# Gate and up products with the tokens as loaded operand and 512 weight columns moving, in a float32 transformer and expert kernel on one core

## The reference

```python
def swiglu(h, w_gate, w_up, w_down):
    return (jax.nn.silu(h @ w_gate) * (h @ w_up)) @ w_down

h = rms_norm(x, norm_g[l, 0])
x = x + 0.5 * swiglu(h, ffn_w_gate[l, 0], ffn_w_up[l, 0], ffn_w_down[l, 0])
```

## Time and profile before

| | us |
|---|---|
| median of 3 runs | 2014.35 |
| lowest, highest run | 2012.62, 2015.29 |
| span of the profiled execution | 2012.0 |
| PE busy, share | 1960.5, 97% |
| DVE busy, share | 1176.1, 58% |
| ACT busy, share | 702.8, 35% |

### The profile page before, as it was taken

How to read it: one execution, slowest core, us unless ns; L and a number is a source line. 1 busy time by engine, 2 the same in 40 slices (tenths; PEclk the granted TensorE clock), 3 DMA queues, 4 the chain that set the end, 5 groups by cost and what they waited for, 6 DMA issues and landing times.

```text
span 2012.0 us, 34328 instructions
## 1 busy us (share of the span) xinstructions
PE 1960.5 (97%) x14457; PEld 1630.7 (81%) x14457; DVE 1176.1 (58%) x2009; ACT 702.8 (35%) x1052; POOL 0.2 (0%) x4
## 2 busy tenths in 40 slices
PE   9999999999999999999999999999899999989997
PEld 9999998889999999999888999999675544444443
DVE  6666659876655765575987757657755422222212
ACT  5433536535333533343653534343322000000001
POOL 0000000000000000000000000000000000000000
PEclk9999999999999999999999999999999999999999
DMA  7799563376776677656325676644318999999995
GB/s 242 243 355 254 173 185 106 118 213 195 219 220 198 208 216 222 193 175 192 116 95 176 207 224 195 206 110 126 126 34 344 401 420 421 421 421 421 421 421 234
DMA packets 274100, 476.17 MB, mean 237 GB/s; under 512 B 28198, under 2 KB 234080, under 8 KB 249368
## 3 DMA queue, kind: packets, MB, share of 16 engines
q1 hardware_dynamic: 273692, 473.85, 68.4%
q10 hardware_dynamic: 252, 0.08, 0.0%
HBM read 472.75 MB, written 7.95 MB: 239 GB/s over the span
## 4 chain that ended last, share of the span: by engine, by line
PE 83%; DMA 11%; DVE 4%; ACT 1%; issue 0%; DVEq 0%; ACTq 0%
PE ps L764 82%; DMA ring_zone<-in_moe_w_up_dram 7%; DMA ring_over<-in_moe_w_up_dram 3%; DMA hT<-in_moe_w_up_dram 1%; PE ps L1095 1%; PE ps L1238 0%; DVE PT L2292 0%; DVE WL L1941 0%; PE ps L1404 0%; DVE xT L2698 0%; DVE hl L1881 0%; ACT mT L1723 0%; ACT gT L1671 0%; DVE gT L2321 0%; DVE gT L2326 0%
## 5 line engine op out<-in xcount | busy, mean ns | idle before, releaser
L1870 DVE TENSOR_TENSOR WL<-W,WH 128x1024 fp32r<-128x1024 f32 x390 | 473.0, 1223 | 310.2 <-ACT WH L1488 309.5
L764 PE MATMUL ps<-hh,WH 128*128 128x256 f32 x2232 | 633.4, 284 | 1.3 <-DVE WL L1870 0.7
L764 PE MATMUL ps<-hh,WL 128*128 128x256 f32 x2232 | 622.6, 279 | 0.0
L764 PE MATMUL ps<-hl,WH 128*128 128x256 f32 x2232 | 622.5, 279 | 0.0
L1488 ACT ACTIVATE WH<-W 128x1024 fp32r<-128x1024 f32 x390 | 408.1, 1055 | 450.1 <-PE ps L764 422.6
L764 PEld LDWEIGHTS ps<-hh,WH 128*128 128x128 f32 x2232 | 418.8, 188 | 14.8 <-issue 11.6
L764 PEld LDWEIGHTS ps<-hl,WH 128*128 128x128 f32 x2232 | 418.4, 187 | 1.2 <-issue 1.0
L764 PEld LDWEIGHTS ps<-hh,WL 128*128 128x128 f32 x2232 | 419.2, 188 | 0.0
L764 PE MATMUL ps<-hid_h,WH 128*128 128x256 f32 x704 | 200.8, 285 | 0.0
L764 PE MATMUL ps<-hid_l,WH 128*128 128x256 f32 x704 | 196.5, 279 | 0.0
L764 PE MATMUL ps<-hid_h,WL 128*128 128x256 f32 x704 | 196.5, 279 | 0.0
(11 more groups left out here) (391 smaller groups left out, 2565.4 us busy)
## 6 DMA issues: line engine op xcount, KB each, us to landing
W<-in_ffn_w_gate_dram SPq DMA_DIRECT2D x88, 512.0 KB, 4.9
W<-in_ffn_w_up_dram SPq DMA_DIRECT2D x88, 512.0 KB, 4.6
W<-in_ffn_w_down_dram SPq DMA_DIRECT2D x88, 512.0 KB, 4.0
W<-in_w_in_dram SPq DMA_DIRECT2D x78, 512.0 KB, 4.6
ring_over<-in_moe_w_gate_dram SPq DMA_DIRECT2D x28, 1024.0 KB, 25.1
ring_over<-in_moe_w_up_dram SPq DMA_DIRECT2D x28, 1024.0 KB, 25.7
ring_over<-in_moe_w_down_dram SPq DMA_DIRECT2D x28, 1024.0 KB, 26.6
W<-in_w_gate_dram SPq DMA_DIRECT2D x48, 512.0 KB, 3.6
```

Of the source, the lines that this page charges most:

```text
L764: ins = nc.tensor.matmul(o, lhsT, rhs, start=start, stop=stop, skip_group_check=True, **kw)
L1870: v.tensor_tensor(low, W[:, i % RAW, :], high.bitcast(F32), ALU.subtract).then_inc(low_ready, 1)
```

## The change

In an FFN the tokens are now the loaded operand of the gate and up products (128 of them at a time, `tt`), and 256 gate columns beside 256 up columns, which lie in two neighbouring places of `WH` and `WL`, are the moving one: 512 columns, one bank for each half of the tokens. The order of pieces in a block becomes gate, up (first half of the width), gate, up (second half). SiLU with the token factor as its scale on ACT and one DVE operation for each half of the tokens make the hidden block with tokens on the partitions; four transposes on PE turn it back into the second bank, between the two halves of the down product of the block before; ACT copies the high part from there, DVE subtracts the rest. The ada products and the others stand behind the transposes. Square root and reciprocal are now of two columns. ACT and DVE split pieces up to fixed numbers (`split_to`).

```diff
+def block_at(b):
+    return 6 * b - 2 if b else 0
...
-                add("ffn_gate", key, b)
-                add("ffn_up", key, b)
+                plan.extend((kind, key, b, half) for half in range(2) for kind in ("ffn_gate", "ffn_up"))
...
+            def rows_of_strips():
+                pe.wait_ge(part_ready, due(part_ready))
+                for tt in range(TT):
+                    mm(ps[:, 1, tt:tt + 1], rs[:, tt * P:(tt + 1) * P], ones[:, 0:1], tt == 0, tt == 1,
+                       then=sum_ready if tt else None)
...
+            def gate_and_up(banks, half, h_wait, then):
+                slot = split_no[st["taken"]] % PAIRS
+                take("ffn_gate")
+                take("ffn_up")
+                for j in range(4):
+                    k = 4 * half + j
+                    if h_wait:
+                        pe.wait_ge(h_ready, due(h_ready))
+                    w = (WH[:, slot:slot + 2, j * 256:(j + 1) * 256], WL[:, slot:slot + 2, j * 256:(j + 1) * 256])
+                    for tt in range(TT):
+                        mm3(banks[tt], h_at(k, tt * P, P), w, k == 0, k == KD - 1, then=then if k == KD - 1 else None)
+                done_pair(2)
+            def turn_hidden_rows(b, bank):
+                pe.wait_ge(hid_rows, due(hid_rows))
+                for f in range(2):
+                    for tt in range(TT):
+                        ins = nc.tensor.transpose(bank[:, f * T + tt * P:f * T + (tt + 1) * P],
+                                                  hid_f[:, b % 2, tt, f * P:(f + 1) * P], ident)
+                ins.then_inc(hid_turned, 1)
...
+                for b in range(FF_BLOCKS):
+                    banks = [begin()]
+                    turns.step()
+                    banks.append(begin())
+                    split_hidden[b] = turns.step()
+                    gate_and_up(banks, 0, b == 0, None)
+                    if b == 0:
+                        squares_by_strip()
+                    if b == 1:
+                        turn_hidden_rows(0, last)
+                    gate_and_up(banks, 1, b == 0, work_ready)
+                    if b == 0:
+                        rows_of_strips()
+                    else:
+                        dve_did(split_hidden[b - 1])
+                        down(b - 1, 0)
+                        turn_hidden_rows(b, banks[1])
+                        side_products(l, i, b)
+                        down(b - 1, 1)
...
 ACT
+                for b in range(FF_BLOCKS):
+                    n = n0 + block_at(b)
+                    split_to(n + 4)
+                    if b == 0:
+                        strips_out()
+                    if b == 1:
+                        hidden_high(0)
+                    split_to(n + 6)
+                    if b == 0:
+                        row_root()
+                        act.wait_ge(row_factor, 2 * l + i + 1)
+                    for tt in range(TT):
+                        bank = look()
+                        turned_bank[b] = turns.bank()
+                        nc.scalar.activation(sg[:, b % 2, tt, :], bank[:, 0:T], ACT.Silu,
+                                             scale=rstd_of[:, tt:tt + 1]).then_inc(sg_ready, 1)
+                        turns.step()
+                    if b:
+                        split_to(n + 7)
+                        hidden_high(b)
+                        split_to(n + 8)
                     if (l, i, b) == (0, 0, LATE_BLOCK + 1):
                         set_up()
...
 DVE
+                for b in range(FF_BLOCKS):
+                    n = n0 + block_at(b)
+                    split_to(n + 4)
+                    if b == 1:
+                        hidden_low(0)
+                    split_to(n + 6)
+                    if b == 0:
+                        row_factors()
+                    for tt in range(TT):
+                        bank = take() if tt == 0 else ps[:, WORK + (turns.n) % WORK, :]
+                        turned_bank[b] = turns.bank()
+                        dve.wait_ge(sg_ready, due(sg_ready))
+                        ins = v.scalar_tensor_tensor(out=hid_f[:, b % 2, tt, :], in0=bank[:, T:2 * T],
+                                                     scalar=rstd_of[:, tt:tt + 1], in1=sg[:, b % 2, tt, :],
+                                                     op0=ALU.mult, op1=ALU.mult)
...
+                    if b:
+                        split_to(n + 7)
+                        hidden_low(b)
+                        split_to(n + 8)
```

More of the change, by code:

```diff
@@ L910, in late_vectors @@
                 turns.step()
-            def ffn(l, i):
[L914 to L949, removed]
@@ new lines, in turn_hidden_rows, with down @@
+            def turn_hidden_rows(b, bank):
[5 more added lines that the diff above has]
+                ins.then_inc(hid_turned, 1)
+            def down(c, f):
+                w = take("ffn_down")
+                hid = at((hid_h[:, c % 2, :], hid_l[:, c % 2, :]), f * T, T)
+                for n in range(KD):
+                    mm3(ps[:, n // 2, (n % 2) * T:(n % 2 + 1) * T], at(w, n * P), hid,
+                        c == 0 and f == 0 and n % 2 == 0, False)
+                done_pair()
@@ new lines, in side_products @@
+            def side_products(l, i, b):
+                if (l, i, b) == (0, 0, LATE_BLOCK):
+                    late_vectors()
+                if ada_unit(l, i, b) is not None:
+                    if ada_unit(l, i, b) == 0:
+                        pe.wait_ge(act_setup, 3)
+                    ada_rows(ada_unit(l, i, b))
+                if ada_unit(l, i, b - 1) is not None:
+                    ada_columns(ada_unit(l, i, b - 1))
+                if (l, i, b) == (1, 1, CONTEXT_AT + 1):
+                    turn_context()
+                if (l, i, b) == (1, 1, CONTEXT_AT + 2):
+                    pe.wait_ge(lrow_ready, 1)
+                    bank = begin()
+                    mm(bank[:, 0:40], ones[0:1, :], lrow[:, :], True, True, then=work_ready)
+                    turns.step()
@@ new lines, in ffn @@
+            def ffn(l, i):
+                last, split_hidden = None, {}
+                for b in range(FF_BLOCKS):
[17 more added lines that the diff above has]
+                        down(b - 1, 1)
+                    last = banks[1]
+                side_products(l, i, FF_BLOCKS)
@@ L1523, in root, with row_root @@
                     .then_inc(rms, 1)
+            def row_root():
+                act.wait_ge(sum_ready, due(sum_ready))
+                nc.scalar.activation(rstd_of[:, :], ps[:, 1, 0:TT], ACT.Sqrt, bias=eps[:, :], scale=1.0 / (32 * D))\
+                    .then_inc(rms, 1)
             def split_to(n):
@@ L1530, in split_to @@
                     high, _, before = split_place(st["split"])
-                    act.wait_ge(pair_used, before + 1)
+                    if before >= 0:
+                        act.wait_ge(pair_used, before + 1)
                     nc.scalar.activation(high, W[:, i % RAW, :], ACT.Copy).then_inc(high_ready, 1)
@@ L1590, in ffn, with hidden_high @@
             def ffn(l, i):
-                for b in range(FF_BLOCKS):
-                    used(2)
+                n0 = st["used"]
+                def hidden_high(b):
+                    act.wait_ge(hid_turned, due(hid_turned))
+                    bank = ps[:, turned_bank[b], :]
+                    nc.scalar.activation(hid_h[:, b % 2, :], bank, ACT.Copy).then_inc(hid_high, 1)
+                turned_bank = {}
+                for b in range(FF_BLOCKS):
+                    n = n0 + block_at(b)
[13 more added lines that the diff above has]
+                                             scale=rstd_of[:, tt:tt + 1]).then_inc(sg_ready, 1)
+                        turns.step()
+                    if b:
+                        split_to(n + 7)
+                        hidden_high(b)
+                        split_to(n + 8)
                     if (l, i, b) == (0, 0, LATE_BLOCK + 1):
                         set_up()
[L1595 to L1604, removed]
                     if (l, i, b) == (0, 0, LATE_BLOCK):
@@ L1614, in ffn @@
                         turns.step()
[L1615 to L1616 removed]
                 turns.step(ada_unit(l, i, FF_BLOCKS - 1) is not None)
[L1618 removed]
+                st["used"] += FFN_PIECES
+                split_to(st["used"] + 2)
             def rows(tile, at, n, src):
```

44 lines of the change are left out of this document (24 added, 20 removed).

## The result

The changed kernel takes 2038.23 us (median of 4 runs, 2036.09 to 2040.13) against 2014.54 of the kernel before in the same job: ratio 1.012, interval 1.0105 to 1.0134. It is 23.7 us slower, where 12.6 faster was forecast.

The account below looks back on a forecast made before the run. TensorE (PE), busy for 97% of the span, was taken as the bound. Terms -41.4 + 19.2 + 1.2 + 4.1 + 4.3 = -12.6 us took the span from 2012.0 to 1999.4; forecast 2001.8 us, 0.6% faster, range 1994 to 2018.

Parts of the forecast that it names:

- Term 1: FFN gate and up products: a 512-column matmul takes 0.216 us for two of 0.1178, 2112 times, -41.4 us.
- rival (a): Gate and up products: the wide matmul gains nothing, 0.236 us each, deciding from 0.222; 2043 us, slower; chance 0.12.
- Term 2: Four PE transposes per FFN block turn the gate-up product: 0.44 us a group, 44 groups, +19.2 us.
- rival (d): PE transposes take their full duration, 0.27 us each, 1.09 per group: +28.8, 2030.6 us, slower; chance 0.03.
- Term 3: Row sums: one fp32 product of 256 columns becomes two of 1 column, +0.3 us four times, +1.2 us.
- Term 4: PE waits for splits in FFN blocks: 0.6 plain, 1.2 at b=1, 1.5 behind set_up, 0.4 on two context blocks; +4.1 us.
- rival (b): Every block waits for turned copy, split and rest, ada blocks too, 0.3 us on 38 or more: 2014, no change; chance 0.13.
- Term 5: Kernel start: first matmul needs both pieces, at 17.0 instead of 13.18; 2.8 us head start lost, +4.3 us in sum.

Follow-up runs that it names:

- the run with one: The changed kernel with one PE transpose per block instead of four, three quarters of the hidden block then holding other numbers: 2024.81 us, ratio 1.0051 to before.
- the earlier start: The changed kernel with both first pieces split ahead of the rounding of x, on ACT and DVE: 2033.85 us, ratio 1.0091 to the kernel before.

## Why the prediction was wrong, point by point

**Term 1 failed**, at the sentence "So I take 0.216". The matmul of 512 columns takes 0.2333; 2112 x (0.2353 - 0.2333) = -4.3 us in place of -41.4. The missing 37.1 is as much as the whole error of 36.4 between the forecast and the measured time. Three things were wrong in it. "Two costs run side by side" left open what a narrow matmul pays beyond the larger of them and took it to vanish at 512 columns. The runs show that a change of weights adds nothing at 512 columns (0.2266, and 0.227 with one tile); and by my estimate float32r pays above its columns there too. What the columns alone take I work out from two stretches at a granted clock of 0.50: 512 columns came 0.427 apart at after's start, and 256 came 0.213 apart in before's trace from 1412.17 to 1414.94. If the distance there goes with the clock, 512 columns take 0.213 at 1.00 (0.417 ns each), my lower bound. The row I chose was of another kind, float32, whose record of 512 columns comes at twice 0.215; float32r pays 13 to 20 ns over 0.213 (0.2267 and 0.2333). And my own pointed to the right answer: the first distance of a float32r row of 128 columns, 0.058 to 0.063 in the trace and 0.06 as shown, is 0.45 to 0.49 ns a column, 0.232 or more at 512. I read it wrongly twice. I put it down to the weights being the same tile; but PE loads that tile again, and within the row the next pair on one tile is 0.11 apart, as the loads are. All 32 such short distances stand behind a 256-column matmul, so I take them for what the columns cost without the load; that is my reading of these times, no run shows it by itself. And I set the 0.06 against rival (a), though four times 0.06 is close to that rival's 0.236, and ranked the float32 row above it "in array time and in weights".

What came is rival (a), "the wide matmul gains nothing", given 0.12: 0.2333 is past its deciding point of 0.222, and its 2043 was 5 us high. The doubt it rested on, something paid per column that I couldn't name, was the better argument.

**Term 2**, +19.2: right. 0.44 a group in after's rows, and 0.10 to 0.11 per transpose by the run with one; rival (d) falls.

**Term 3**, +1.2: 0.1. The new sums lengthen PE's row by 0.45 for each FFN, from the product before them to the second behind; the old one did by 0.43.

**Term 4**, +4.1: 4.8, near by luck. 2.8 of it is 0.32 + 1.17 + 0.42 + 0.68, and 0.2 more at a wait in the context's products that the kernel before has too. Plain blocks and `set_up` came near what was worked out (0.3 and 1.5 forecast), blocks with an ada product don't wait, so rival (b) falls. But the four waits at b=1 (1.2) did not come, and the three in block 0 (2.0), which the prediction put at nothing, did: the same need for two split pieces at once that it saw at the very start holds at the second half product too.

**Term 5**, +4.3: mis-sized. No run shows the 1.5 that this sum has beside the 2.8; in its place after's start had 12 matmuls at a granted clock of 0.50, 0.427 apart instead of 0.2333, which cost 2.3. PE's first product came at 17.80, not 17.0: with the head start of 2.8 that is 5.9, and undoing it put the trace 6.3 ahead (the median 4.4).

The terms as measured give -4.3 + 19.2 + 0.1 + 4.8 + 5.9 = 25.7. The narrow matmuls that remain take back 1.8: their mean is 0.1171 for 0.1177 in the down products (1.2 us) and 0.1169 for 0.1171 in the attention products with x moving (0.6); why they shift so isn't shown. That leaves 23.9, and after's trace is 24.6 behind at the end of the last FFN, so all but 0.7 is accounted for. The span rose by only 22.8 because in before's trace the last transposes have an idle of 1.67 us among them and then run at a granted clock of 0.50 (2003.1 to 2004.9), and in after's there is neither (1.00 from 2024.9 to 2027); the change doesn't touch them. PE's timelines of before, then of after:

```profile
2003.09 1.75 PE L1461 MATMUL ps<-C,xT 128*128 128x128 f32 x7 [1.67 <-issue]
...
2024.93 1.97 PE L1516 MATMUL ps<-C,xT 128*128 128x128 f32 x16 [0.91 <-DVE xT L2798]
```

What stays open: by which rule the two operands' places set 227, 233 or 240 ns, and what sends a row of 256 columns to 113 or to 118. A kernel in which x lies like the weights for the gate and up products alone was not tried; from its parts (2038.2 - 4.4 - 5.8 - 12) it would be at 2016 by this estimate, not below before.

## What to carry to other kernels

Take a matmul's distance from rows of its own type: one of float32 (0.43 for a record of 512 columns) or bfloat16 (0.216) didn't tell that of float32r (0.227 to 0.240), and halving the count of matmuls saved 2.0 ns of 235 here, since the cost went with the columns. When the engine that bounds the kernel gets new work (here four transposes a block), the saving that pays for it has to be measured by itself first; ten lines put in front of the kernel would have shown it. A step that wants two split pieces at once has to be looked at wherever it occurs: the prediction did so at the start and missed it in the next three FFNs. And before two layouts of a float32r kernel are compared, look at the distances of matmuls that were not touched: moving tiles by 64 bytes cost the kernel before as much here as the whole change.

## What was not expected of the hardware

- float32r of 512 columns took 226.7, 233.3 or 240 ns depending on the relative place of its two operands, bfloat16 216; loading the same tile each time (227), or only 64 columns of it (230), made it no faster.
- Moving the split weights by 64 bytes made the kernel before 24 us slower, 9,800 matmuls of 256 columns going from 117.5 to 119.9 ns, and the wide ones of the change faster by 5.8 ns.
- A row of 24 matmuls of 256 columns ran at 113.3 or at 118 ns with the same operands and nothing else running, in nine of the ten rows of one run from start to end; two rows that differed in this way had one small product ahead of them and two.
- Behind the same idle of PE near 1450 (4.14 us in after's trace, 4.13 in the other) the granted clock fell in both traces (0.57 from 1456 to 1460 in after's, 0.50 from 1452 to 1456 in that of the earlier start); over the 10 us that followed it was 1.00 in the first and 0.54 in the second. Together with one such stretch of 3 us that took back 6 us, more than most edits here.
